# VectorE's order within a projection: the next block's low part ahead of a modulation's piece

## What is computed

```python
def adaln_modulation(c, w, b):
    mod = jax.nn.silu(c) @ w + b              # c: (1, 1024), w: (1024, 6144)
    return [m[:, None, :] for m in jnp.split(mod, N_MOD, axis=-1)]

for layer in range(DEPTH):
    shift_m, scale_m, gate_m, shift_f, scale_f, gate_f = adaln_modulation(c, *ada[layer])
    h = rmsnorm(x, pre_m) * (1.0 + scale_m) + shift_m
    x = x + gate_m * rmsnorm(mixers[layer](h), post_m)      # starts with h @ w_in
    h = rmsnorm(x, pre_f) * (1.0 + scale_f) + shift_f
    x = x + gate_f * rmsnorm(swiglu(h, *ffns[layer]), post_f)
```

## Time and profile before

| | |
|---|---|
| median of 3 runs | 1981.85 us (1978.69 to 1981.88) |
| profiled execution | 1975.85 us |
| its span, first to last instruction | 1974.1 us |
| TensorE busy | 1886.5 us (96%) |
| VectorE busy | 1444.2 us (73%) |
| ScalarE busy | 993.4 us (50%) |
| GpSimd busy | 258.5 us (13%) |
| mean granted clock of TensorE | 0.991 |

### The profile page before, as it was taken

One profiled execution on the slowest core, in us unless ns is written; L12 is line 12 of the kernel. 1 busy time (PEld: TensorE's weight loads), 2 busy tenths in 40 slices (PEclk: granted clock), 3 DMA queues, 4 the chain that ended last, 5 costly groups with the idle time before them and its releaser, 6 DMA issues.

```text
span 1974.1 us, 31980 instructions
## 1 busy us (share of the span) xinstructions
PE 1886.5 (96%) x12506; PEld 1702.2 (86%) x12506; DVE 1444.2 (73%) x2618; ACT 993.4 (50%) x1442; POOL 258.5 (13%) x118
## 2 busy tenths in 40 slices
PE   6999899999989899999999899999999999999998
PEld 6887799999968788889898799999988888888886
DVE  5898775558957785557666559888878887777776
ACT  5655544455435554454555546566643334444444
POOL 0001044430001044430000175000000000000000
PEclk8999999999999999999999999999999999999999
DMA  8764376756464255546444344577767766465452
GB/s 317 241 206 150 139 267 244 268 205 218 170 238 147 96 203 192 191 151 220 149 150 167 114 168 172 187 215 216 216 206 261 301 235 231 174 233 194 175 208 108
DMA packets 94549, 391.88 MB, mean 199 GB/s; under 512 B 7680, under 2 KB 41776, under 8 KB 56000
## 3 DMA queue, kind: packets, MB, share of 16 engines
q1 hardware_dynamic: 94112, 389.58, 55.8%
q10 hardware_dynamic: 288, 0.26, 0.1%
HBM read 371.72 MB, written 15.73 MB: 196 GB/s over the span
## 4 chain that ended last, share of the span: by engine, by line
PE 76%; DVE 13%; ACT 3%; issue 2%; DMA 1%; POOL 0%; ACTq 0%; DVEq 0%; SPq 0%
PE ps L582 9%; PE acc L566 9%; PE acc L568 9%; PE acc L567 9%; PE ps L570 6%; PE ps L572 5%; PE ps L571 5%; PE ps L583 5%; PE acc L570 3%; PE acc L571 3%; PE acc L572 3%; DVE wlo L1399 2%; PE ps L1354 1%; PE acc L1354 1%; DVE arena L1428 1%
## 5 line engine op out<-in xcount | busy, mean ns | idle before, releaser
L2488 ACT ACTIVATE whi<-raw 128x1024 fp32r<-128x1024 f32 x557 | 588.4, 1059 | 448.9 <-PE acc L568 223.9
L1399 DVE TENSOR_TENSOR wlo<-raw,whi 128x1024 fp32r<-128x1024 f32 x461 | 560.7, 1223 | 283.2 <-ACT whi L2488 280.1
L570 PE MATMUL ps<-hpair,whi 128*128 128x256 f32 x1104 | 318.1, 288 | 10.5 <-DVE wlo L1399 6.2
L1399 POOL TENSOR_TENSOR wlo<-raw,whi 128x1024 fp32r<-128x1024 f32 x96 | 241.3, 2516 | 608.8 <-ACT whi L2488 608.5
L571 PE MATMUL ps<-hpair,whi 128*128 128x256 f32 x1104 | 313.0, 283 | 0.0
L572 PE MATMUL ps<-hpair,wlo 128*128 128x256 f32 x1104 | 312.9, 283 | 0.0
L566 PE MATMUL acc<-whi,chi 128*128 128x512 f32 x752 | 297.2, 395 | 3.4 <-DVE wlo L1399 1.9
L568 PE MATMUL acc<-wlo,chi 128*128 128x512 f32 x752 | 294.7, 392 | 0.0
L567 PE MATMUL acc<-whi,clo 128*128 128x512 f32 x752 | 294.1, 391 | 0.0
L582 PE MATMUL ps<-hpair,whi 128*128 128x512 f32 x800 | 284.5, 397 | 0.8 <-DVE hpair L1514 0.8
L570 PEld LDWEIGHTS ps<-hpair,whi 128*128 128x128 f32 x1104 | 212.2, 192 | 15.0 <-issue 4.9
(11 more groups left out here) (455 smaller groups left out, 2949.1 us busy)
## 6 DMA issues: line engine op xcount, KB each, us to landing
raw<-in_peer_down SPq DMA_DIRECT2D x64, 1024.0 KB, 4.9
raw<-in_peer_up SPq DMA_DIRECT2D x64, 1024.0 KB, 5.0
arena<-in_ada SPq DMA_DIRECT2D x80, 512.0 KB, 5.0
raw<-in_w_gate SPq DMA_DIRECT2D x22, 1024.0 KB, 4.8
raw<-in_w_up SPq DMA_DIRECT2D x22, 1024.0 KB, 4.8
raw<-in_w_down SPq DMA_DIRECT2D x22, 1024.0 KB, 4.8
arena<-spill SPq DMA_DIRECT2D x14, 1024.0 KB, 6.9
spill<-hT_t SPq DMA_DIRECT2D x22, 448.0 KB, 6.3
```

The costliest lines, as they stand in the source:

```text
L570: e.matmul(out, hi, xh, start=start, stop=False, skip_group_check=True)
L1399: e.tensor_tensor(out=lo, in0=w, in1=hi.bitcast(F32), op=ALU.subtract).then_inc(*X(("lo", j)))
L2488: e.activation(hi, w, ACT.Copy, scale=1.0).then_inc(*self.A(("hi", j)))
```

## The change

ve_linear and its sibling for token-major outputs, ve_linear_tok, call cut_lo once more, ahead of the piece, up to last+1. The low part of block last+1 is made there; the call behind the piece then has only last+2 to make. The other engines' lists are as before. Where a linear carries no piece, or block last+1 has been made already or isn't VectorE's, the order of VectorE's instructions is unchanged.

```diff
     def ve_linear(self, e, name, i, kt, nn, eager=False, ada=True):
+        self.cut_lo(e, self.V, self.W.last(name, (i + 1) * nn * kt - 1) + 1)
         if ada:
             self.ve_ada(e)
         if eager:
...
     def ve_linear_tok(self, e, name, i, kt, ada=True):
+        self.cut_lo(e, self.V, self.W.last(name, (i + 1) * kt - 1, 256) + 1)
         if ada:
             self.ve_ada(e)
         self.ve_cuts(e, name, (i + 1) * kt - 1, 256)
```

## The result

The changed kernel takes 1987.14 us (median of 10 runs, 1983.38 to 1989.88) against 1978.72 us (10 runs, 1975.42 to 1981.88): ratio 1.0043, 95% interval [1.0032, 1.0055], or 6.3 to 10.9 us more. The forecast was 7.5 us more. The forecast of the time was counted from 1981.85 us, the median of before's first three runs; that of all ten lies 3.1 us lower. The profiled execution of after took 1988.22 us with a span of 1986.4, 12.3 us over before's. The two profiles overstate the distance: before's lies 2.9 us under its median, after's 1.1 us over.

The account below looks back on a forecast made before the run. VectorE was taken to set the pace of w_xbc and w_z, TensorE that of the feed-forward layer. The terms 6.88 + 0.5 + 0.5 - 0.4 = 7.5 us, added to 1981.85 us, gave 1989 us, range 1981 to 1994 us.

Parts of the forecast that it names:

- The main step: In w_xbc, linears 2 to 5, VectorE would idle for ScalarE's high part where the piece stood: 5.95 us lost.
- the clock: At linear 2 of w_xbc, TensorE's new wait for a piece may lower its clock and delay conv steps: 0.5 us.
- w_xbc, linears 2 to 5: VectorE loses 1.54 us in each of three linears and 1.33 us in linear 2: 5.95 us.
- w_z, first linear: VectorE comes before the first high part is ready and idles 0.93 us that the pieces filled.
- w_z from the second linear on: The high part is early there, so low parts and pieces take the same time in either order: no cost.
- Entry of the first feed-forward layer: The piece there ends later, and TensorE waits some 0.5 us for it.
- Gains: In the gated stage one linear waited 0.43 us for its first low part: 0.4 us back.
- The waits that were to vanish: TensorE's 2.06 us wait for a low part before w_xbc's linear 1 goes, but the time saved has no taker.
- Faster: Rival: waits for low parts go and nothing replaces them; 5.5 us less, 1976 us; chance 0.10.
- Absorption: No-change rival: the stalls come, but later slack takes them; about 1982 us; chance 0.09.
- Slower still: Rival: new waits keep TensorE at the lower clock through w_xbc's linears 2 to 5; 8.8 us more, 1998 us; chance 0.07.

Follow-up runs that it names:

- swap_warm: The change plus idle matmuls in TensorE's two long waits, ahead of linear 2 of w_xbc and the first linear of w_z; 1979.32 us, ratio to before 1.0011.
- swap_hi_first: The change, with ScalarE making the first of its two high parts in w_xbc ahead of its conv-step wait and SiLU; 1979.21 us, ratio to before 1.0013.
- no_piece: Before's order, with the pieces of w_xbc's linears 2 to 5 moved to the output projection w_out0a; 1982.67 us, ratio to before 1.0031.
- wz_only: Before with the swap in w_z alone; 1979.90 us, ratio to before 1.0011.
- xbc_only: Before with the swap in the six linears of w_xbc alone; 1986.26 us, ratio to before 1.0048.
- gated_only: Before with the swap in the gated stage alone (w_gqk, w_gg, w_nq and w_gv); 1975.77 us, ratio to before 0.9987.
- hi_first: Before's order on VectorE, with ScalarE's first high part of w_xbc made ahead of SiLU; 1977.79 us, ratio to before 1.0008.
- not_xbc: Before with the swap everywhere but in w_xbc; 1979.66 us, ratio to before 1.0012.
- xbc_from2: Before with the swap in linears 2 to 5 of w_xbc alone; 1984.18 us, ratio to before 1.0034.

## Why the prediction was right, step by step

The time, 1987.14 us, is inside the range and 1.9 us from the forecast; 8.4 us was measured for 7.5. The main step was right in mechanism and size. That the sum came so near is partly luck. Up to the end of w_z the sum has 6.88 us and 0.5 for the clock, 7.4 together, where the traces show 10.9: the clock was mis-sized by 3.4 us. The median shows less of that than the traces do, and what took the difference is not shown. And 1989 us was counted from a median 3.1 us above the later one.

- **w_xbc, linears 2 to 5 (5.95 us): right.** VectorE's new waits are 1.64, 1.65, 1.64 and 1.65 us, of which 0.40 us was there before: 6.18 us. In swap_warm, without the lower clock behind the long waits, w_xbc loses 5.97 us. The turn was to be 7.9 us and is 8.02. swap_hi_first and no_piece show the cause from both sides.
- **w_z, first linear (0.93 us): right.** The wait is 1.54 us where 0.50 us was the earlier trace rows: 1.04 us. In swap_warm w_z adds 1.06 us.
- **w_z from the second linear on (free): wrong.** I asked only whether the high part is early. In the change the second linear's low part waits 0.47 us and then takes 2.26 us at 129.08, because GpSimd multiplies from 128.35 to 130.26: 1.5 us. The swap puts a low part where GpSimd's work can meet it, and the slow linear ahead of it, behind which ScalarE and so GpSimd are late, decides which one: in swap_warm no low part is held; in wz_only the second low part of that linear is, without a slow clock in w_z. Before, those low parts stood behind the pieces and met nothing. GpSimd's work was in no step of the prediction.
- **The clock (0.5 us): mis-sized, 3.9 us with the meeting that it brought about, 2.3 us at linear 2 alone.** The late piece, the wait of nearly 4 us and the lower level behind it came as told. But TensorE got the piece at 82.17 us where I had 81.7, at that level the modulation's matmuls took 1.73 us (linear 2 starts at 83.90) where I had 0.9, and linear 2 took 7.6 us where I had 7.3. It ended at 91.5, not at 90.0 us, and the conv steps waited 1.83 us instead of 0.5. And the same wait comes a second time, 3.24 us ahead of w_z's first linear, for the piece of w_xbc's linear 5, which I did not look at: xbc_only, without the swap in w_z, loses 2.3 us there. The Trainium skill's rule (TensorE: Matmul & The Clock Gate, HAM oscillation) was worth more here than I gave it: not in every turn, but behind both long waits the clock was 0.50, while behind the 2.04 us wait at 106.59 it was 1.00.
- **Entry of the first feed-forward layer (0.5 us): right**, 0.64 us at 261.12.
- **Gains (0.4 us): too small.** In the change TensorE loses two waits in the gated stage, 0.43 us for a low part and 0.70 us for ScalarE's eviction; of these has the first, and I had counted only waits that name a low part. In time gated_only puts the gain at 0.02 to 0.24%.
- **The waits that were to vanish** did, in part: the 2.06 us wait is 0.87 us, and no time came of it, since VectorE arrives at the conv steps no earlier. The slow clock behind it belonged to that execution of before: the eight kernels here that keep before's order at this place wait 0.92 to 2.51 us, and none has the lower clock behind it.
- **The rivals.** Faster fell where it decides, at w_xbc; where its condition held, in the gated stage, it was true. Absorption fell in the change: its distance behind w_z stays to the end (in swap_warm the output projection took 3.6 us back). "Slower still" came true for two linears, not for a row of them. The end of w_z was to come some 7 us later and came 11.3 us later.

Profiles and medians differ by 4 us here. The terms from the profile of the change (0.4 us ahead of w_xbc, 8.3 in w_xbc, 2.6 in w_z, then +1.0 net) make 12.3 us, and the medians say 8.4, with an interval that ends at 10.9. One part can be named, because before's profiled execution was a quick one: between 206 and 241 us the distance grows from 11.4 to 13.3 us, as the granted clock falls once more in the change's execution (at 217.5 us) than in before's. gated_only and hi_first, which have no edit there, fall back by 1.9 and 1.8 us at the same place, so this part belongs to before's profile and not to the change. The other 2 us stay open.

## What to carry to other kernels

Before moving a step ahead of another on a busy engine, ask when its input is ready and what the engine did until then: here the piece of 1.54 us filled, to within 0.02 us, the wait for a high part that comes through VectorE's own result, and moving it turned filler into a second wait. Then ask who needs the step that moved back: TensorE waited 3.83 us for it, and the lower clock behind the wait cost more than the lateness: with the wait filled, nothing waited for linear 2. An order that loses where a loop between two engines sets the pace can still gain where inputs are early; choose it by stage.

## What the runs showed of the hardware

VectorE and GpSimd held each other here when both worked on tensors in SBUF. A low part of 1.22 us took 2.93 us when it started 0.12 us after GpSimd's multiplication, and ended 1.1 us after it; a multiplication of 1.9 us took 2.81 us at 114.79, 0.18 us behind the start of another low part. In before the same multiplication, at 124.35, ran beside operations that read a bank, and neither grew: 1.90 us, and 0.68 us for each subtraction. The Trainium skill (SBUF — State Buffer, Who interferes with whom) calls the ports that the two engines share an exclusive lock, and says that a VectorE instruction with two inputs in SBUF contends with a GpSimd instruction that reads SBUF. These traces agree: the low part reads two tensors in SBUF, the subtraction one.

Waits of TensorE of nearly the same length were followed by different clocks: 2.06 us at 73.58 in before by 0.61, and 2.51 us at 71.90 in not_xbc, ahead of the same linear, by 1.00; 2.04 us at 106.59 in the change by 1.00, and 2.04 us at 101.66 in xbc_from2, ahead of the same linear, by 0.50 (102 to 105 us).
